# Held weight pieces loaded from GpSimd's queue, a new table of steps for the w_mod products and the high parts, and the first diagonals made by ScalarE

## The reference

```python
c_act = silu(c)
for layer in range(2):
    mod = c_act @ w_mod[layer] + b_mod[layer]
    shift, scale, gate = split(mod, 3)
    hdn = rms_norm(x, norm_w[layer]) * (1 + scale) + shift
    q1, k1, v1, g1, q2, k2, v2, g2 = split(hdn @ w_in[layer], 8)
    # layer 0: y1 differential attention, y2 dilated attention
    # layer 1: y1 causal attention over one block, y2 stick-breaking attention
    y = concat([y1 * silu(g1), y2 * silu(g2)]) @ w_out[layer]
    x = x + gate * y
```

## Time and profile before

| | |
|---|---|
| median of three runs | 338.74 us (338.22 to 339.8) |
| profiled execution, time of its own | 338.16 us |
| its span | 336.4 us |
| PE busy | 303.1 us, 90% |
| DVE busy | 234.1 us, 70% |
| ACT busy | 196.3 us, 58% |
| POOL busy | 13.2 us, 4% |
| moved from memory | 68.95 MB |

### The profile page before, as it was taken

One profiled execution on the slowest core, in us unless ns is written; L12 is line 12 of the kernel. 1 busy time (PEld: TensorE's weight loads), 2 busy tenths in 40 slices (PEclk: granted clock), 3 DMA queues, 4 the chain that ended last, 5 costly groups with the idle time before them and its releaser, 6 DMA issues.

```text
span 336.4 us, 4790 instructions
## 1 busy us (share of the span) xinstructions
PE 303.1 (90%) x1709; PEld 239.4 (71%) x1709; DVE 234.1 (70%) x482; ACT 196.3 (58%) x399; POOL 13.2 (4%) x20
## 2 busy tenths in 40 slices
PE   2498988999989599996999999999999999988895
PEld 2487766776555468883565888889888789887684
DVE  3899998879783865567867647879774535469533
ACT  4524487555565836993534454675654886997400
POOL 0000000000005323000000000000000000000000
PEclk9999999999999979997999999999999999999999
DMA  6999998573687484089982505587556146000011
GB/s 254 373 417 406 406 406 330 186 242 104 228 306 267 162 322 187 2 274 415 320 278 94 179 5 187 187 311 241 205 185 253 64 152 222 27 36 2 0 64 62
DMA packets 19879, 70.31 MB, mean 209 GB/s; under 512 B 2192, under 2 KB 2576, under 8 KB 19856
## 3 DMA queue, kind: packets, MB, share of 16 engines
q1 hardware_dynamic: 19856, 70.01, 57.4%
HBM read 68.95 MB, written 1.05 MB: 208 GB/s over the span
## 4 chain that ended last, share of the span: by engine, by line
PE 66%; DVE 12%; ACT 9%; DMA 8%; issue 3%; SPq 1%; ACTq 0%; DVEq 0%
PE proj L1075 45%; PE score L1075 12%; DMA raw<-in_w 6%; PE mixed L1075 4%; DVE w_lo L746 3%; DVE raw L766 2%; DMA raw<-in_w_mod 2%; PE turned L1120 2%; PE turned L1102 2%; ACT w_hi L476 2%; DVE probs L1019 1%; ACT logits L687 1%; ACT logits L685 1%; ACT logits L683 1%; DVE xs L961 1%
## 5 line engine op out<-in xcount | busy, mean ns | idle before, releaser
L746 DVE TENSOR_TENSOR w_lo<-raw,w_hi 128x1024 fp32r<-128x1024 f32 x68 | 82.4, 1221 | 16.6 <-ACT w_hi L476 16.2
L476 ACT ACTIVATE w_hi<-raw 128x1024 fp32r<-128x1024 f32 x68 | 70.8, 1051 | 20.6 <-DMA raw<-in_w 19.5
L1075 PE MATMUL proj<-w_hi,hy_hi 128*128 128x512 f32 x144 | 60.5, 420 | 9.7 <-DVE hy_lo L800 5.1
L766 DVE CUSTOM_DVE_ANT_0 raw<-raw,c_rows 128x1024 f32<-128x1024 f32 x48 | 57.8, 1222 | 4.5 <-DMA raw<-in_w_mod 4.5
L1075 PE MATMUL proj<-w_hi,hy_lo 128*128 128x512 f32 x144 | 57.4, 398 | 0.0
L1075 PE MATMUL proj<-w_lo,hy_hi 128*128 128x512 f32 x144 | 57.1, 397 | 0.0
L1075 PE MATMUL proj<-hy_hi,w_hi 128*128 128x256 f32 x176 | 52.5, 298 | 0.0
L1075 PE MATMUL proj<-hy_lo,w_hi 128*128 128x256 f32 x176 | 49.7, 282 | 0.0
L1075 PE MATMUL proj<-hy_hi,w_lo 128*128 128x256 f32 x176 | 49.7, 282 | 0.0
L1075 PEld LDWEIGHTS proj<-w_hi,hy_hi 128*128 128x128 f32 x144 | 27.7, 192 | 18.1 <-DVE hy_lo L951 5.8
L1075 PEld LDWEIGHTS proj<-hy_hi,w_hi 128*128 128x128 f32 x176 | 33.5, 191 | 2.1 <-issue 2.1
(11 more groups left out here) (144 smaller groups left out, 428.0 us busy)
## 6 DMA issues: line engine op xcount, KB each, us to landing
raw<-in_w SPq DMA_DIRECT2D x76, 512.0 KB, 4.8
raw<-in_w_mod SPq DMA_DIRECT2D x48, 512.0 KB, 6.1
xs<-in_x SPq DMA_DIRECT2D x1, 1024.0 KB, 5.3
qT<-in_w SPq DMA_DIRECT2D x2, 512.0 KB, 4.0
kT<-in_w SPq DMA_DIRECT2D x2, 512.0 KB, 6.4
out_x<-xs SPq DMA_DIRECT2D x4, 256.0 KB, 2.0
cst<-in_constants SPq DMA_DIRECT2D x1, 520.0 KB, 6.3
logits<-in_a_lambda SPq DMA_DIRECT2D x1, 128.0 KB, 11.8
```

Of the source, the lines that this page charges most:

```text
L476: nc.scalar.activation(w_hi[:, slot(n), :, :], raw_tile(("w", n)), ACT.Copy).then_inc(hi_done, 1)
L746: nc.vector.tensor_tensor(w_lo[:, slot(n), :, :], raw_tile(("w", n)), w_hi[:, slot(n), :, :], ALU.subtract).then_inc(lo_done, 1)
L766: nc.vector.tensor_tensor_reduce(out=tile, in0=tile, in1=c_rows[:, :], scale=1.0, scalar=0.0, op0=ALU.mult, op1=ALU.add, accum_out=col(V_M ...
L1075: return nc.tensor.matmul(o, a, b, start=start, stop=stop, skip_group_check=True)
```

## The change

Four things are changed.

1. The four held pieces are issued by GpSimd, at the end of its stream, behind a wait for step 59. SP no longer waits for that step.
2. `MOD_AT` is written out: tiles m17 to m39 stand at other steps. m17 to m35 come earlier than before where the steps differ, up to step 46 three tiles more than before; none stand at 47 to 49, 52, 54 to 56, 60, 62, 64, 65 and 67.
3. In `EARLY` the high parts of the pieces 28 to 33 and 35 are made later: 28 at step 43 (was 42), 29 at 45 (44), 30 at 48 (46), 31 at 50 (48), 32 at 52 (49), 33 at 54 (51), 35 at 55 (53). The low parts stay one step behind. The list of loads follows from these numbers.
4. The two diagonals at the top are made by ScalarE (a Copy with a scale for each partition), which waits for VectorE's factor.

```diff
-EARLY = {24: 14, 27: 16, 28: 14, 29: 13, 30: 12, 31: 11, 32: 15, 33: 14, 35: 14, 36: 10}
+EARLY = {24: 14, 27: 16, 28: 13, 29: 12, 30: 10, 31: 9, 32: 12, 33: 11, 35: 12, 36: 10}
...
-MOD_AT = [25 + 2 * i for i in range(24)] + [STEPS + 16 + 3 * i for i in range(8)]
+MOD_AT = [25, 26, 28, 29, 30, 33, 35, 37, 38, 41, 42, 43, 45, 46, 50, 51, 53, 57, 58, 59, 61, 63, 66, 68] + [STEPS + 16 + 3 * i for i in range(8)]
...
             for i, key in enumerate(loads):
-                if key == behind_held:
-
-                    wait_step(sp, HELD_FROM)
-                    for n, b in zip(HELD, held):
-                        sp.dma_start(b, w[n].rearrange("p (k n) -> p k n", k=2)).then_inc(held_in[HELD.index(n)], 16)
...
             rms_seed(x_ms[:, 0:2], x_y[:, 0:2], x_t[:, 0:2], x_ln, x_seed, x_seed2, 1)
+            act.wait_ge(x_rms, 1)
+            for t in range(2):
+                nc.scalar.activation(x_diag[:, t, :], ident, ACT.Copy, scale=x_t[:, t:t + 1]).then_inc(diag_ok, 1)
             first_blocks(0)
...
             refine(x_ms[:, 0:2], x_y[:, 0:2], x_t[:, 0:2]).then_inc(x_rms, 1)
-            dve.wait_ge(x_rms, 1)
-            for t in range(2):
-                x_diagonal(t)
...
+            wait_step(pool, HELD_FROM)
+            for i, n in enumerate(HELD):
+                nc.gpsimd.dma_start(held[i], w[n].rearrange("p (k n) -> p k n", k=2)).then_inc(held_in[i], 16)
```

More of the change, by code:

```diff
@@ L395, in program @@
         later += [(at - 1, 0, ("mod", m)) for at, m in zip(MOD_AT, LATER_MODS)]
-        later.sort()
-        loads += [key for _, _, key in later]
-        behind_held = next(key for at, _, key in later if at > HELD_FROM)
+        loads += [key for _, _, key in sorted(later)]
         place = {key: i for i, key in enumerate(loads)}
```

## The result

The changed kernel takes 326.88 us (median of four executions, 326.37 to 327.57), the kernel before 339.27 beside it on the same chip; the ratio is 0.9635, 95% interval 0.9594 to 0.9675. Forecast were 326.9. The profiled execution took 326.71 us, its span is 324.9.

The account below looks back on a forecast made before the run. Only TensorE's pauses could be won, TensorE being busy 303.1 of 336.4 us. From the profiled 338.16, -7.2 + 1.25 - 5.0 - 0.85 gives 326.36; with 0.58 for the median, 326.9 us, 8-in-10 range 324.8 to 331.8.

Parts of the forecast that it names:

- Place 1: TensorE's wait for piece 25 ahead of step 50, and half clock behind it, go: -7.2 us up to step 51.
- Place 2: ScalarE without slack at pair 6's turned maps; later high parts make TensorE wait there: +1.25 us, between 0 and 2.6.
- Place 3: Steps 60 to 66: no load waits behind SP's wait for step 59, VectorE's chain ends earlier: -5.0 us (-5.6 to -3.1).
- Place 4: TensorE's wait for the diagonal at the turn goes, as pass m39 comes earlier: -0.85 us, at worst 0.
- The top: Start of the kernel, diagonals made by ScalarE: 0, between -0.4 and +0.2 us, the transfer deciding.
- A: Rival: ScalarE and VectorE give more back and the clock falls at pair 6, 331.2 us; chance 0.16 together with D.
- B: Rival: no change, piece 25 and the w_mod tile late anyway, only 1.6 us of issue time saved, 337.1 us; chance 0.06.
- C: Rival: slower, GpSimd's queue lands its four transfers one after another, 342.1 us at 9 us each; chance 0.07.
- D: Rival at piece 25: it waits at another slot, some 3 us lost again, ending like A; chance 0.16 together with A.

Follow-up runs that it names:

- e1b: Kernel before with only the four held loads moved to GpSimd's queue, run once more for its profile: 333.86 us.
- e3: Kernel before with only its top changed, both diagonals made by ScalarE: 338.34 us against 338.26, ratio 0.9994.
- e4: Changed kernel with the high part of piece 35 one step earlier, at step 54: 325.89 us.
- e7: As e4, with the high part of piece 36 also moved from step 58 to 64: 325.17 us, ratio to the kernel before 0.9597.
- e5: Kernel before with the held loads on GpSimd and the new MOD_AT, EARLY as before: 328.03 us, ratio 0.9691.
- e2: Kernel before with only both tables changed, SP still issuing the held pieces: 330.76 us, ratio 0.9763.
- e6: Kernel before with the held loads on GpSimd and the new EARLY, MOD_AT as before: 327.83 us, ratio 0.9686.
- a0: The changed kernel run again unaltered, on the same chip as later experiments, as their base: 326.93 us.
- e1: Kernel before with only the four held loads moved to GpSimd's queue, first run: 333.93 us, ratio 0.9859.
- e9: Changed kernel with GpSimd's wait in front of the held loads at step 62 instead of 59: 326.73 us.
- e8: Changed kernel with the four held loads issued by SP again, behind the wait for step 59, in front of piece 40: 326.60 us.

## Why the prediction was right

- **Place 1** (-7.2): shown by e1b and by the timeline. From the scores behind step 46 to step 51 the time fell from 15.28 (108.02 to 123.30) to 8.61, so -6.67. The term failed in one count: I put steps 48 and 49 at 24 matmuls of 0.12 us from 110.30 and so 5.3 us of waiting, where PE's timeline has 4.78 (the second of these matmuls starts 0.52 behind the first and not 0.12). That is the whole of the miss against this one profile; in e1b and e3 the same stretch took 16.47 and 16.20 us, and against them place 1 is worth 7.9 and 7.6.
- **Place 2** (+1.25): +0.93 from step 51 to step 60 (138.72 here, 144.31 before). The two pauses of 0.55 and 0.91 us, both released by ScalarE, are those forecast, but shorter than the 1 to 1.6 us there; the clock stayed. e4 and e7 show that the high parts of pieces 35 and 36 cause them, and e5, with the high parts where they were, has only the 0.61 of the kernel before.
- **Place 3** (-5.0): -4.70. The mechanism is shown by e1b and e2. Its size hangs on the clock: from pair 6's second turned map to step 66 the profile of the kernel before takes 16.65 us (144.04 to 160.69), e3 15.57 (145.64 to 161.21), the changed kernel 11.95. So the 1.5 us put down to matmuls at half speed come off in some executions only, and against e3 place 3 is worth 3.62. VectorE's second low part ended at 147.96, forecast 147.45. But steps 64 and 65 had two limits within 0.2 us of each other: step 64 started at 146.64 right behind the turned map at 146.37, whose copy comes from ScalarE, and step 65 at 148.11 right behind step 64, when its low part had been there for 0.15 us. The prediction named VectorE alone, and here it is not VectorE that comes last. e7, which relieves ScalarE, started step 66 1.67 us earlier within its own interval, 0.72 more than e4.
- **Place 4** (-0.85): -1.01 from step 66 to the turn (16.23 before, 15.22 now). 0.85 is the pause; the rest is that without one the turn starts 0.16 us ahead of the modelled end of the matmul in front (165.39 + 0.39 against 165.62). e6 shows that the pass moved by `MOD_AT` does it.
- **The top** (0): shown by e3.
- **Behind the turn** almost nothing changed: 159.48 us to the end of the span before, 159.28 now.
- The misses have both signs (+0.5, -0.3, +0.3, -0.15), and so the sum is nearer than its terms deserve: 326.36 against the profiled 326.71. That the median was hit within 0.1 us is luck besides: I added 0.58 for the distance of median and profile, and in the changed kernel it is 0.17. The gain between the medians is 12.39 us, between the profiled executions 11.45. The kernel before scatters more (337.05 to 340.75 in the runs beside the experiments, the changed one 326.34 to 327.57 in a0), which fits a clock that does not fall alike in each execution.
- **Rivals.** A did not come: no clock fell at pair 6. B is refuted twice: the held loads alone give 3.9 to 4.5 us (e1b, e1), and e2 has piece 25 in time. C did not come: piece 34 could have landed 12.5 us after its issue (137.85 to 150.40), and landed within 7.0. The last of the four, piece 39, landed within 10.6 us of its issue, by 150.8 at the latest, and was wanted at 158.41. D did come, but in e5 only: one piece further on, for 1.62 us.

On the bound for C, the prediction cited the Trainium skill (SBUF — State Buffer, "Who interferes with whom"): VectorE's plain tensor-tensor operations don't lock out descriptor generation. The trace agrees as far as it goes: the four issues took 2.3 us on GpSimd, 0.53 to 0.73 each, in a window in which VectorE was busy 2.29 of 2.40 us (137.80 to 140.20 above). No run has them beside an idle VectorE, so the rule itself is not tested.

## What to carry to other kernels

Look in the queue's own waits for a load that stands long for a compute step, and ask who is queued behind it: what costs is not the wait but what it keeps back, and a later place in the same queue cures it as well as a second queue. In a ring of slots, a piece is late because of who had its slot before; a change of any table moves all of these pairs, so list predecessor and time of release for the next two pieces also, not only for the one that was late. And when a stall is removed, take the engine that is unbroken in the next stretch and move the largest deferrable operation out of it; this gave the last 1.7 us.

## What the runs showed of the hardware

- Pauses of PE of 0.85 to 1.62 us left the granted clock at 1.00 behind them; pauses of 2.29, 3.20 and 4.78 were followed by 0.73, 0.59 and 0.50 in the windows right behind. But behind the 3.14 of e3 it stayed at 1.00. So with pauses of 2.29 to 3.20 us the length alone does not tell what the clock does. I had only 0.85 and 2.95 to go by. At the top the record is not enough: behind a pause of 3.83 the window from 10.80 to 14.00 shows 1.00, and yet eight matmuls take 2.05 us where the same eight take 1.05 at 165.62. Timeline of PE in the changed kernel:

```profile
10.80 2.05 PE L1072 MATMUL turned<-x_diag,xs 128*128 128x128 f32 x8 [3.83 <-ACT x_diag L514]
```

- The same four loads landed, from GpSimd's queue, after 6.7 and 9.6 us (medians of `qT` and `kT`, changed kernel), 4.1 and 6.8 (e1b), 4.6 and 6.8 (e9), and from SP's at nearly the same moment (e8) after 5.4 and 7.1. GpSimd's were 1.3 and 2.5 us later there. Between kernels the landing from GpSimd's one queue moved by up to 2.8 us, which is more. That other loads in flight do this is a guess; no run tries it.
- VectorE's pass over w_mod and GpSimd's bias operations slow each other, and in these rows the one that starts second pays. Timelines of the changed kernel:

```profile
119.91 1.75 DVE L761 CUSTOM_DVE_ANT_0 raw<-raw,c_rows 128x1024 f32<-128x1024 f32 x1
```
```profile
118.88 1.70 POOL L1062 TENSOR_TENSOR qn<-qn,cst 128x256 f32<-128x256 f32 x1
120.55 1.38 POOL L1060 TENSOR_SCALAR qn<-cst 128x256 f32<-128x256 f32 x1
```

and of VectorE in the kernel before, where the pass starts ahead of the add at 124.24 and keeps its 1.22:

```profile
124.14 1.22 DVE L766 CUSTOM_DVE_ANT_0 raw<-raw,c_rows 128x1024 f32<-128x1024 f32 x1
```

Three passes of the changed kernel take 0.53 us more each (at 106.98, 119.91 and 122.93). It cost nothing, PE having no pause from step 48 to pair 6, but a sum that counts such a pass at 1.14 would be short where VectorE has no idle time.
